# Expert stage of a fused block: every weight unit split, silu on ScalarE, unused slots left out

## What is computed

```python
g_top_p, g_top_i = lax.top_k(g_prob, 1)          # one of 4 groups
top_val, top_idx = lax.top_k(e_logits, 2)        # two of its 8 experts
weights = g_top_p * jax.nn.softmax(top_val, axis=-1)
...
def expert_block(args):
    xblk, e = args
    h = jax.nn.silu(xblk @ w_gate[e]) * (xblk @ w_up[e])
    return h @ w_down[e]
...
y = jnp.zeros((T + 1, D), f32).at[buf_tok].add(yb.astype(f32) * buf_w[:, None])[:T]
```

## Time and profile before

| quantity | value |
|---|---|
| time, median of 3 (range) | 2327.53 us (2326.26 to 2328.1) |
| profiled execution: its time | 2324.4 us |
| profiled execution: its span in the trace | 2322.7 us |
| TensorE busy | 2122.0 us, 91% of the span |
| VectorE / ScalarE / GpSimd busy | 1233.8 / 905.8 / 201.9 us |
| bytes moved by DMA | 378.64 MB |

### The profile page before, as it was taken

One profiled execution on the slowest core, in us unless ns is written; L12 is line 12 of the kernel. 1 busy time (PEld: TensorE's weight loads), 2 busy tenths in 40 slices (PEclk: granted clock), 3 DMA queues, 4 the chain that ended last, 5 costly groups with the idle time before them and its releaser, 6 DMA issues.

```text
span 2322.7 us, 28282 instructions
## 1 busy us (share of the span) xinstructions
PE 2122.0 (91%) x10907; PEld 1098.6 (47%) x10907; DVE 1233.8 (53%) x1374; ACT 905.8 (39%) x1219; POOL 201.9 (9%) x264
## 2 busy tenths in 40 slices
PE   7988989898499999999946999959999999999999
PEld 5445446644244544454413565534444444444444
DVE  5234247644688888888867253384533343333432
ACT  5212227623376676667644242372312111211210
POOL 1000130000111111111130000032000000000000
PEclk9999999999699999999977999979999999999999
DMA  8201310052399999999975152234212121011101
GB/s 327 114 36 37 91 28 1 19 202 82 138 416 422 423 417 417 412 415 415 389 277 213 38 180 87 79 102 164 73 37 72 36 72 37 36 72 36 36 0 73
DMA packets 77021, 378.64 MB, mean 163 GB/s; under 512 B 12368, under 2 KB 19152, under 8 KB 44368
## 3 DMA queue, kind: packets, MB, share of 16 engines
q1 hardware_dynamic: 54000, 296.82, 32.5%
q0 software_dynamic: 22944, 80.75, 9.9%
HBM read 326.67 MB, written 37.75 MB: 157 GB/s over the span
## 4 chain that ended last, share of the span: by engine, by line
PE 86%; DVE 7%; issue 2%; DMA 2%; SPq 1%; ACT 1%; POOL 1%; POOLq 0%; DVEq 0%; ACTq 0%
PE ps L409 22%; PE ps L410 22%; PE ps L411 22%; PE pt L1974 5%; PE pt L409 2%; PE pt L410 1%; PE pt L411 1%; PE pt L1928 1%; DVE cols L1445 1%; PE pt L463 1%; SPq L922 1%; PE pt L2030 1%; PE pt L2032 1%; PE pt L2031 1%; PE pt L1864 1%
## 5 line engine op out<-in xcount | busy, mean ns | idle before, releaser
L409 PE MATMUL ps<-xt,split 128*128 128x512 f16 (+1 forms) x992 | 372.9, 376 | 17.1 <-issue 9.4
L409 PE MATMUL ps<-split,xt 128*128 128x512 f16 x928 | 354.4, 382 | 26.0 <-DMA xt<-arena 19.9
L410 PE MATMUL ps<-xt,split 128*128 128x512 f16 (+1 forms) x992 | 372.5, 376 | 0.0
L411 PE MATMUL ps<-xt,split 128*128 128x512 f16 (+1 forms) x992 | 372.5, 375 | 0.0
L410 PE MATMUL ps<-split,xt 128*128 128x512 f16 x928 | 354.4, 382 | 0.0
L411 PE MATMUL ps<-split,xt 128*128 128x512 f16 x928 | 354.0, 381 | 0.0
L548 DVE SCALAR_TENSOR_TENSOR split<-stage,split 128x2048 f16<-128x2048 f32 x128 | 290.0, 2287 | 56.3 <-ACT split L544 56.3
L544 ACT ACTIVATE split<-stage 128x2048 f16<-128x2048 f32 x128 | 237.5, 1902 | 122.0 <-PE ps L411 120.9
L409 PE MATMUL ps<-split,arena 128*128 128x512 f16 x512 | 194.3, 379 | 0.0
L410 PE MATMUL ps<-split,arena 128*128 128x512 f16 x512 | 194.3, 379 | 0.0
L411 PE MATMUL ps<-split,arena 128*128 128x512 f16 x512 | 194.3, 379 | 0.0
(11 more groups left out here) (292 smaller groups left out, 3010.7 us busy)
## 6 DMA issues: line engine op xcount, KB each, us to landing
stage<-in_w_gate SPq DMA_DIRECT2D x64, 1024.0 KB, 7.8
stage<-in_w_up SPq DMA_DIRECT2D x64, 1024.0 KB, 8.1
arena<-in_w_down SPq DMA_DIRECT2D x64, 1024.0 KB, 10.0
stage<-in_w_mlp SPq DMA_DIRECT2D x32, 1024.0 KB, 6.2
y_rows<-arena POOLq DMA_DIRECT2D x48, 512.0 KB, 8.3
arena<-in_conv_taps POOLq DMA_DIRECT2D x32, 576.0 KB, 4.2
stage<-in_w_dense_a SPq DMA_DIRECT2D x16, 1024.0 KB, 8.5
stage<-in_w_dense_b SPq DMA_DIRECT2D x12, 1024.0 KB, 10.1
```

What stands on the lines that cost most here:

```text
L409: nc.tensor.matmul(out_ap, lh, rh, start=start, stop=False)
L410: nc.tensor.matmul(out_ap, lh, rl, start=False, stop=False)
L411: return nc.tensor.matmul(out_ap, ll, rh, start=False, stop=stop)
```

## The change

In the expert loop unit 5 is loaded and split like the others (`native`, `hTf` and the L1974 product are gone), ScalarE computes silu in one activation, and ScalarE writes both halves of y. The gather and the store of an expert use index columns in which an unused slot has an index out of range, and the DMA leaves such rows out. The store scatters each row to row k * 1024 + token of `y_rows` (k is 0 or 1), so that the combine loads whole blocks, issued by SyncE. The router writes the first two index columns itself, and VectorE waits with the first remainders until the first two gathers are issued. The early zeroing of `y_rows` is gone; a memset of the gather tiles stands in its place, ahead of the first gather.

```diff
         xn_rows = nc.dram_tensor("xn_rows", (S, D), F32, kind="Internal").ap()
-        y_rows = nc.dram_tensor("y_rows", ((BLK_MAX + 1) * P, D), F32, kind="Internal").ap()
+        y_rows = nc.dram_tensor("y_rows", (2 * S, D), F32, kind="Internal").ap()
         x2_rows = nc.dram_tensor("x2_rows", (S, D), F32, kind="Internal").ap()
...
-        def native(q):
-
-            return AR[:, 2048:4096] if q == 0 else AR[:, 6144:8192]
-
-        def expert_load(sp, kind, e, q=None):
+        def expert_load(sp, kind, e):
...
                 src = a["w_" + kind][bass.ds(2 * e + i, 1), :, :].rearrange("o p c -> (o p) c")
-                if s == 5:
-                    if not (isinstance(e, int) and e < 2):
-                        sp.wait_ge(s_d[1], e - 1)
-                    sp.dma_start(native(q), src).then_inc(s_wn[q], 16)
-                    continue
                 if not (isinstance(e, int) and BASE[s] + e == 0):
...
             if not (isinstance(e, int) and e == 0):
-                act.wait_ge([s_u, s_u, s_g, s_g, s_d[0]][s], e)
+                act.wait_ge([s_u, s_u, s_g, s_g, s_d[0], s_d[1]][s], e)
             nc.scalar.activation(whi(s), wstage(s), ACT.Copy, scale=WS).then_inc(s_wh[s], 1)
...
             ch.done(V_.tensor_tensor(rblk, rv, rix, ALU.add))
-            V_.scalar_tensor_tensor(out=slot, in0=rblk, scalar=float(P), in1=rpos, op0=ALU.mult, op1=ALU.add)
-
             V_.tensor_tensor(rA, io.unsqueeze(1).to_broadcast([P, 2 * TT, P]),
...
                 i = V_.tensor_tensor(rB[:, k * TT:(k + 1) * TT, :], rB[:, k * TT:(k + 1) * TT, :],
-                                     bc(tok, BLK_MAX + 1), ALU.mult)
+                                     bc(row[:, k, :], BLK_MAX + 1), ALU.mult)
             i.then_inc(s_rt, 1)
...
+            dve.wait_ge(s_rp, 3)
+            rows = PS[:, 0, 0:BLK_MAX + 1]
+            ch.done(V_.tensor_scalar(rsec, rows, -float(S), -float(S), ALU.is_ge, ALU.mult))
+            V_.scalar_tensor_tensor(out=idx2, in0=rows[:, 0:2], scalar=2.0 * S, in1=rsec[:, 0:2],
+                                    op0=ALU.add, op1=ALU.add)
+            V_.scalar_tensor_tensor(out=tok_of, in0=rows, scalar=2.0 * S, in1=rsec, op0=ALU.add, op1=ALU.add)\
+                .then_inc(s_slots, 1)
+            V_.tensor_scalar(dest_of, rows, 2.0 * S, None, ALU.add)
             ch.done(V_.tensor_tensor(rov[0:1], rinc[0:1, :].unsqueeze(1).to_broadcast([1, NOVER + 1, NE]),
...
             V_.tensor_scalar(over_e, rbe[0:1, :], float(NE - 1), None, ALU.min)
-            V_.tensor_copy(n_over, rinc[0:1, NE - 1:NE])
-            dve.wait_ge(s_rp, 3)
-            V_.tensor_copy(tok_of, PS[:, 0, 0:BLK_MAX + 1]).then_inc(s_slots, 1)
+            V_.tensor_copy(n_over, rinc[0:1, NE - 1:NE]).then_inc(s_slots, 1)
...
                 load_b(sp, m)
+            sp.wait_ge(s_moe, 1)
+            for t in range(TT):
+                if t >= 4:
+                    sp.wait_ge(s_cmb, 2 * (t - 3))
+                for k in range(2):
+                    sp.dma_start(YG[t % 4][k], y_rows[k * S + t * P:k * S + (t + 1) * P, :]).then_inc(s_yg[t % 4], 16)
...
-            pool.wait_ge(s_zero, 1)
-            pool.wait_ge(s_xl, TT)
-            for b in range(NE, BLK_MAX + 1):
-                pool.dma_start(y_rows[b * P:(b + 1) * P, :], zero).then_inc(s_cleared, 16)
...
                 pool.wait_ge(s_xs[i], 16 * TT // 2)
+            pool.wait_ge(s_lg, 1)
+            nc.gpsimd.memset(XTF[:, 0:2048], 0.0).then_inc(s_rows, 1)
+            pool.wait_ge(s_rows, 1)
             pool.wait_ge(s_slots, 1)
...
-                nc.gpsimd.tensor_copy(idx[q], tok_of[:, bass.ds(e, 1)]).then_inc(s_ix, 1)
-                pool.wait_ge(s_ix, e + 1)
-                pool.sem_inc(s_seen, 1)
+                if not (isinstance(e, int) and e < 2):
+                    nc.gpsimd.tensor_copy(idx[q], tok_of[:, bass.ds(e, 1)]).then_inc(s_ix, 1)
+                    pool.wait_ge(s_ix, e - 1)
+                    pool.sem_inc(s_seen, 1)
                 pool.indirect_dma_start(out=XG[q], out_offset=None, in_=xn_rows,
-                                        in_offset=bass.IndirectOffsetOnAxis(ap=idx[q], axis=0))\
-                    .then_inc(s_gx[q], 16)
+                                        in_offset=bass.IndirectOffsetOnAxis(ap=idx[q], axis=0),
+                                        bounds_check=S - 1, oob_is_err=False).then_inc(s_gx[q], 16)
...
                 pool.wait_ge(s_y[1], e + 1)
-                dst = y_rows[bass.ds(e * P, P), :]
-                pool.dma_start(dst, y[q]).then_inc(s_ys[q], 16)
+                nc.gpsimd.tensor_copy(dst[q], dest_of[:, bass.ds(e, 1)]).then_inc(s_sx, 1)
+                pool.wait_ge(s_sx, e + 1)
+                pool.sem_inc(s_seen, 1)
+                pool.indirect_dma_start(out=y_rows, out_offset=bass.IndirectOffsetOnAxis(ap=dst[q], axis=0),
+                                        in_=y[q], in_offset=None,
+                                        bounds_check=2 * S - 1, oob_is_err=False).then_inc(s_ys[q], 16)
...
             gather(1, 1)
+            pool.sem_inc(s_gi, 1)
+            pool.wait_ge(s_slots, 2)
             pool.wait_ge(s_xt, 1)
...
-            for t in range(TT):
-                if t >= 4:
-                    pool.wait_ge(s_cmb, 2 * (t - 3))
-                for k in range(2):
-                    pool.indirect_dma_start(out=YG[t % 4][k], out_offset=None, in_=y_rows,
-                                            in_offset=bass.IndirectOffsetOnAxis(ap=slot[:, k, t:t + 1], axis=0))\
-                        .then_inc(s_yg[t % 4], 16)
+            pool.sem_inc(s_moe, 1)
...
+                    act.wait_ge(s_h, e)
+                nc.scalar.activation(tbuf, PS[:, q, :], ACT.Silu, scale=IWS).then_inc(s_t, 1)
                 if not (last and q):
...
                 act.wait_ge(s_ht, e + 1)
+                if not (first and q == 0):
+                    act.wait_ge(s_d[1], e)
                 nc.scalar.activation(hTh, PS[:, 3, :].rearrange("p (k t) -> p k t", k=4), ACT.Copy)\
                     .then_inc(s_hh, 1)
-                if not (first and q == 0):
-                    act.wait_ge(s_d[1], e)
-                nc.scalar.activation(hTf, PS[:, 3, :].rearrange("p (k t) -> p k t", k=4), ACT.Copy)\
-                    .then_inc(s_hf, 1)
                 if not last:
+                    expert_hi(act, 2, e + 2)
                     xe_hi(e + 2, q)
-                    for s in (2, 3):
-                        expert_hi(act, s, e + 2)
+                    expert_hi(act, 3, e + 2)
                 act.wait_ge(s_d[0], e + 1)
...
                     expert_hi(act, 4, e + 1)
+                act.wait_ge(s_d[1], e + 1)
+                nc.scalar.activation(y[q][:, 512:1024], PT[:, 3, :], ACT.Copy, scale=IWS).then_inc(s_y[1], 1)
+                if not (last and q):
+                    expert_hi(act, 5, e + 1)
...
+            dve.wait_ge(s_gi, 1)
             for i in range(2):
...
             def body(e, q, first, last):
-                dve.wait_ge(s_es, e + 1)
-                nc.vector.scalar_tensor_tensor(out=tbuf, in0=PS[:, q, :], scalar=IWS, in1=sig,
-                                               op0=ALU.mult, op1=ALU.mult).then_inc(s_t, 1)
                 dve.wait_ge(s_u, e + 1)
...
                                                op0=ALU.mult, op1=ALU.mult).then_inc(s_h, 1)
+                expert_lo(dve, 5, e)
                 if not (last and q):
...
                 dve.wait_ge(s_hh, e + 1)
-                dve.wait_ge(s_hf, e + 1)
                 nc.vector.tensor_tensor(hTl, PS[:, 3, :].rearrange("p (k t) -> p k t", k=4), hTh, ALU.subtract)\
...
                         expert_lo(dve, s, e + 2)
-                dve.wait_ge(s_d[1], e + 1)
-                if not (first):
-                    dve.wait_ge(s_ys[q], 8 * e if q == 0 else 8 * (e - 1))
-                nc.vector.tensor_copy(y[q][:, 512:1024], PT[:, 3, :]).then_inc(s_y[1], 1)
                 if not (last and q):
...
                 pe.wait_ge(s_hl, e + 1)
-                pe.wait_ge(s_wo[4], BASE[4] + 1 + e)
-                if not (first and q == 0):
-                    pe.wait_ge(s_y[0], e)
-                for k in range(UK):
-                    c = slice(k * UC, k * UC + UC)
-                    m = product(pe, PT[:, 2, :], hTh[:, k, :], hTl[:, k, :], whi(4)[:, c], wlo(4)[:, c],
-                                k == 0, k == UK - 1)
-                m.then_inc(s_d[0], 1)
-                pe.wait_ge(s_hf, e + 1)
-                pe.wait_ge(s_wn[q], 16 if first else 8 * (e - q) + 16)
-                if not (first and q == 0):
-                    pe.wait_ge(s_y[1], e)
-                for k in range(UK):
-                    m = nc.tensor.matmul(PT[:, 3, :], hTf[:, k, :], native(q)[:, k * UC:k * UC + UC],
-                                         start=k == 0, stop=k == UK - 1)
-                m.then_inc(s_d[1], 1)
+                for i in range(2):
```

(4 more changed lines are left out.)

51 lines of the change are left out of this document (31 added, 20 removed).

## The result

The changed kernel takes 2310.84 us (median of 4 executions, 2306.1 to 2313.16); before, on the same chip, 2327.82 (4 executions, 2326.26 to 2330.31). The ratio is 0.9923, with a 95% interval from 0.9903 to 0.9943: faster, by 17 us, where 37.5 were forecast, and the time lies 2.8 us above the range.

The account below looks back on a forecast made before the run. TensorE was taken to bound the expert loop. Savings of 26.9 (loop), 7.5 (ahead) and 3.1 (behind) sum to 37.5 us: 2324.4 becomes 2286.9, and with the median 3.1 above, 2290 us; range 2282 to 2308.

Parts of the forecast that it names:

- behind: From y(31) to the combine: earlier remainders, scatter and direct loads save 3.1 us, bounds 0 and 3.6.
- ahead of the loop: From the router's last result to gate(0): earlier, smaller gathers bring gate(0) to 610.1, saving 7.5 us, 4.4 with slow landing.
- loop: Expert loop: an expert takes 16.85 us instead of 17.69, 0.84 us x 32 = 26.9 us saved.
- The step that failed: DMA in the expert loop: half-size gather and store leave 6.82 MB per 16.85 us, 404 GB/s, so it keeps up.
- The DMA becomes the bound: Rival, expert loop: unused slots cost what used ones do, 17.4 us per expert, 9 us saved, time 2308; 10%.
- TensorE's price of the split: Down in the expert loop: 12 float16 matmuls at 2.59 us replace the float32 product at 3.43 us.
- VectorE and ScalarE keep up: Expert loop: VectorE's work 16.0 us, ScalarE's 14.1 (14.7 with dearer Silu), both below TensorE's 16.85 us.
- VectorE becomes the bound: Rival, expert loop: VectorE keeps 2.3 us idle on 15.5 us of work, 17.8 us per expert, time 2321; 10%.
- the issue adds 1: GpSimd in the expert loop: issuing the store's indirect DMA takes 1 us, with no cost to the time.
- DMA share below 1: Expert loop's profile: a sign that the forecast is right; a share still at 1 with ScalarE waiting would speak against it.
- VectorE stands still until both gathers are out: Ahead of the loop: VectorE waits while gather 0 is done at 601.3 and gather 1 at 602.6.
- y + 12: Behind the loop: the combine was taken to start 12 us after y(31) is written, against 14.3 before.

Follow-up runs that it names:

- e11_best: Changed kernel with remainders of x(0) and x(1) ahead of those of units 0 and 1, no wait for the gathers, used slots on even partitions: 2291.67 us.
- e9: Changed kernel with only the slots' places permuted, so that used slots stand on the even partitions: 2296.12 us, ratio 0.9869.
- e14: Changed kernel with used slots in groups of eight, but the other groups in partitions 32 to 63 and 96 to 127: 2293.72 us.
- e10: Changed kernel with used slots placed on every second group of eight partitions: 2310.16 us, ratio 0.9934.
- e13: Changed kernel with used slots placed on every second group of four partitions: 2311.32 us, ratio 0.9934.
- e6: Changed kernel with index limits so low that practically every slot is left out, `y_rows` zeroed early: 2296.64 us, ratio 0.988.
- e7_16slots: Changed kernel gathering and scattering only the first 16 slots of each block, `y_rows` zeroed early: 2290.48 us, ratio 0.9853.
- e1_full: Changed kernel with nothing left out; unused slots gather a valid row and write it to a spare one: 2310.71 us, ratio 0.9939.
- e8: Kernel before plus only the row part of the change: slots left out, scatter, whole loads of y, early gathers: 2320.61 us, ratio 0.9988.
- e4: Changed kernel with VectorE kept still until the rows of both first gathers have landed: 2309.91 us, ratio 0.9924.
- e5: Changed kernel without VectorE's wait, remainders of x(0) and x(1) put ahead of those of units 0 and 1: 2309.59 us, ratio 0.993.
- e2: Changed kernel gathering and scattering only the first 64 slots of each block, `y_rows` zeroed early: 2300.25 us, ratio 0.9897.
- e3: Changed kernel storing y as a block of 128 rows, as before the change, instead of scattering: 2310.86 us, ratio 0.9937.
- e12: Kernel before plus only six split units, silu and both y halves on ScalarE; rows as before: 2310.58 us, ratio 0.9943.

## Why the prediction was wrong, step by step

The terms, in us of the profiled executions (before to changed, before to e11_best); the stretches are bounded by gate(0), the end of y(31) and the start of the combine, and the 0.83 us wait inside the combine counts to "behind":

| term | forecast | changed | e11_best |
|---|---|---|---|
| ahead of the loop, 617.59 to gate(0) | 7.5 | 3.6 | 7.1 |
| loop, 569.7 before | 26.9 | 8.4 | 25.4 |
| behind, to the combine's second tile | 3.1 | 2.7 | 2.7 |
| after that | 0 | -3.1 | 0.2 |
| span | 37.5 | 11.6 | 35.3 |

**The step that failed** is in the paragraph on the DMA: "Half of the slots are unused, so a gather and a store move half: 6.29 + 0.52 = 6.82 MB in 16.85 us, 404 GB/s, below the 413 to 421 that the rows sustain". The bytes were right, 12.67 MB on q0 instead of 25.43. The conclusion was not, since the 16 engines do not share them: all used rows lay on eight engines, which had as much to do as with full blocks, while eight had less. A load of a unit is, as I read it, spread over all 16 and complete only when the slowest is: it landed after 11.4 to 12.2 us, and after 7.2 to 7.8 us in e9. The loop paid for it: it gave 8.4 us instead of 26.9, and 25.4 with the slots spread. The last 1.5 us I did not look into. Shown by e9 and e14 against e10 and e13, in which only the place of the slots differs. The sentence behind it, "I take nothing" for an unused slot, was right in itself (9 ns in e6).

**A rival had the number.** "The DMA becomes the bound" gave 17.4 us per expert and 2308 us, and the changed kernel has 17.46 and 2310.84. Its mechanism was still wrong: "an unused slot costs the queues what a used one does" is refuted by e6, whose slots are all left out and whose loop runs at TensorE's pace. It came to the right size by luck, because the full blocks and the fullest engine of the changed kernel carry the same 459 KB. The low chance that I gave it, 10%, rested on "skipped rows have no bytes", which is true and did not matter.

**TensorE's price of the split** was right: 16.85 us between x transposes once the DMA is relieved (e11_best), 2.59 us for 12 matmuls instead of 3.43.

**VectorE and ScalarE keep up**: right. With the DMA relieved TensorE is busy for 60.00 of 60 us, with VectorE at 56.0 and ScalarE at 49.4 in the mean of e9's seven stretches. Per expert that is 15.7 and 13.9 us, where 16.0 and 14.1 were forecast (the rival's 15.5 us for VectorE's work has no working; with 16.0 it would have come to 18.3 us per expert). Silu takes 0.58 us, and in the loop there is no table load. The rival "VectorE becomes the bound" falls: in the changed kernel VectorE's waits that matter (L1554 for L1212) begin with a load that ScalarE waits for. That "the issue adds 1" on GpSimd was too low: in the changed kernel's loop a gather's issue takes 2.26 us in the median and a scatter's 2.17, but nothing waits for them.

**The sign that I named for a full DMA was a poor one.** "DMA share below 1" was to show the forecast right; it is 0.98 to 1.00 in the changed kernel and 0.99 in e7_16slots, where nothing waits. What separates them is ScalarE's wait for loads (73 us against none) and the time to landing (11.4 to 12.2 us against 7.3 to 7.4). The packets hint at why the share says so little: it seems to count an engine's waiting in the middle of a packet as busy. A weight packet of 8 KB takes 309 to 313 ns in the median; what such packets take beyond 309 adds up to 0.9% of the 16 engines' time in e1_full, 5.9% in the changed kernel and 9.4% in e6_skip_all. Without it the changed kernel's share is 0.93, that of e6 0.89. Read so, the contradiction of above, full queues at 391 GB/s, is gone: part of the engines had time to spare. No run tests this reading by itself.

**Ahead of the loop**: "VectorE stands still until both gathers are out" failed. The semaphore after the two gathers was counted while by the profile the second was not yet issued, and its issue ran against the two remainders, 4.64 us. The wait held nothing up: in e8, which doesn't have it, VectorE starts 0.67 us after the first gather's issue too (601.45 and 600.78). e4 and e5 show both ways around; only the second, which also takes the remainders off x's way, gives the forecast 7 us. The landing of the first gather was as taken: from the end of its issue to x(0)'s transposes 3.1 us, 2.7 forecast.

**Behind the loop**: y + 12 was right within half a us, and the wait of the second tile is gone. A table load of 1.28 us that I had not foreseen stands ahead of the four high parts (L582): VectorE starts its remainders 3.6 us after y, not 2.6.

**After the combine** the changed kernel loses 3.1 us and e11_best nothing, with the same code. TensorE's granted clock from 1260 to 1360 us is 0.93 in the one, and 0.97 in the other's corresponding stretch, 1238 to 1338 (before: 0.96, 1273 to 1373):

```profile
1260.00:1360.00 100.00, 95.51 (x547) 55.45 (x548) 29.75 (x43) 28.06 (x44) 4.84 (x9) 0.93 0.23 70
```

It lies in the execution as much as in the kernel: from the combine to the end e6_skip_all takes 1123.3 us and e7_16slots 1117.5, and they differ only in their rows. Over all profiled executions the stretch falls into two groups, 1117.5 to 1118.5 us in seven (e1, e2, e3, e7, e8, e10, e13) and 1123.1 to 1123.8 in six (changed, e4, e5, e6, e9, e14), with before, e11 and e12 between them. What decides it stays open, and a difference of 6 us between two single profiled times can be this alone. It stays open too whether the even partitions or the mixed eights are the better place; their intervals overlap.

## What to carry to other kernels

Count a transfer's bytes per DMA engine, not in total: rows that are left out at one end of the partitions relieve only the engines that serve that end, and every load spread over all engines then waits for the fullest ones. Where an expert or a block is half full, spread its used slots over the partitions; here one permuted operand took off 12 to 15 us (by the ratios and by the medians of e9_spread and the changed kernel), where leaving out half of the rows had taken off none. To see a full DMA, look at who waits for loads and how long a load takes to land; the DMA share can stand at 0.99 in a loop that never waits, and where the engines do wait for loads, a rate below one that the same kernel has reached is a sign of a lopsided load (391 GB/s against 422). Without such waits it is none: e6 and e7 run at 374 and 381.

## What the runs showed of the hardware that I had not expected

- A slot that an indirect transfer leaves out is still a packet, of under 512 B: 3077 more of them in 420 us than with full blocks. 7200 packets of q0 with 0.04 MB took 1.0% of the queues' time, 9 ns each (e6).
- A gather and a scatter over 128 partitions behave as if each engine served two fixed groups of four partitions, 32 apart, also when half of the slots are left out (e13 2311.32, e14 2293.72).
- The DMA held 422 GB/s for 420 us (e1_full, e12_units_only).
- On GpSimd, a semaphore increment that stands behind an indirect DMA in the program was counted before that DMA's issue started: VectorE, waiting for it, ran from 600.73, the issue began at 601.46 by the profile. And the issue of one of the first two gathers, 0.96 to 1.09 us otherwise, took 4.64 to 4.71 us beside two remainders of VectorE, in all eleven runs in which they met. In the changed kernel's loop, where VectorE is busy for 54 of 60 us, an issue takes 2.2 to 2.3 us in the median.
- Behind a loop with Silu stands a table load of 1.28 us ahead of the next high parts (changed kernel and e12), though inside the loop Silu and Copy alternate with none; behind the loop with the sigmoid (before, e8) there is none.
- A packet's recorded length seems to include its engine's waiting: 8 KB packets, 309 to 313 ns in the median, pass 1 us in more than one of a hundred in the changed kernel and e6, and 99 of 100 stay under 0.33 us in e1_full.
